# Down product of the experts' class of 112 rows: weights stationary in halves of 64 columns instead of rows stationary

## The reference, cut to what matters

```
act = clamped_swiglu(xb @ w_gu[e] + b_gu[e])     # xb: rows of the tokens of expert e
return act @ w_dn[e] + b_dn[e]                   # the "down product" is act @ w_dn[e]
```

## Time and profile before

| | us |
|---|---|
| median of 3 runs (2195.15 to 2198.58) | 2197.89 |
| profiled execution | 2196.53 |
| its span, first to last instruction | 2194.9 |
| TensorE busy | 2136.4 (97%) |
| VectorE busy | 995.7 (45%) |
| GpSimd busy | 596.6 (27%) |
| ScalarE busy | 383.1 (17%) |

### The profile page before, as it was taken

The page is one execution under the profiler, slowest core; times in us unless marked ns, Lnnn a source line. Parts: engine busy times, 40 slices in busy tenths (PEclk is TensorE's granted clock), DMA queues, the critical chain, the costliest instruction groups (busy, mean ns, idle before and its releaser), DMA issues.

```text
span 2194.9 us, 50020 instructions
## 1 busy us (share of the span) xinstructions
PE 2136.4 (97%) x20106; PEld 1655.6 (75%) x20106; DVE 995.7 (45%) x2147; ACT 383.1 (17%) x785; POOL 596.6 (27%) x905
## 2 busy tenths in 40 slices
PE   8999999999799999999999999899999999999998
PEld 5555566544488878788787789798999999999443
DVE  4665467445754434444344332623233333343474
ACT  3120066401411111011111100100000000000344
POOL 0466678200123131221311311213111232212420
PEclk9999999999899999999999999999999999999999
DMA  5100011411299999999999984988666888885740
GB/s 208 44 26 6 6 59 45 182 58 67 104 387 416 419 415 358 353 358 340 341 335 336 336 295 171 374 329 340 249 224 240 293 307 313 312 315 190 263 171 39
DMA packets 101814, 528.15 MB, mean 241 GB/s; under 512 B 22327, under 2 KB 26215, under 8 KB 49615
## 3 DMA queue, kind: packets, MB, share of 16 engines
q1 hardware_dynamic: 76894, 465.58, 56.7%
q0 software_dynamic: 24816, 61.12, 7.9%
HBM read 496.06 MB, written 27.30 MB: 238 GB/s over the span
## 4 chain that ended last, share of the span: by engine, by line
PE 91%; DVE 3%; issue 3%; ACT 2%; DMA 1%; POOL 1%; POOLq 0%; DVEq 0%; SPq 0%; ACTq 0%
PE ps L1958 23%; PE ps L1955 20%; PE ps L1971 10%; PE ps L1994 10%; PE ps L1693 5%; PE ps L2031 3%; PE ps L1984 3%; PE ps L1798 3%; PE ps L1682 3%; PE ps L1805 2%; PE ps L1644 1%; PE ps L1712 1%; PE ps L1778 1%; PE ps L1746 1%; PE ps L1677 1%
## 5 line engine op out<-in xcount | busy, mean ns | idle before, releaser
L1958 PEld LDWEIGHTS ps<-xT,wg 128*64 128x64 f32 x10752 | 498.4, 138 | 27.1 <-issue 27.1
L1958 PE MATMUL ps<-xT,wg 128*64 128x112 f32 (+5 forms) x10752 | 503.7, 257 | 12.4 <-issue 9.1
L1955 PE MATMUL ps<-xT,wg 128*128 128x144 f32 (+5 forms) x3072 | 434.8, 304 | 0.0
L1955 PEld LDWEIGHTS ps<-xT,wg 128*128 128x128 f32 x3072 | 430.0, 190 | 4.5 <-issue 1.3
L1507 DVE TENSOR_SCALAR gb<-ps,bcur 128x256 f32<-128x256 f32 x264 | 127.6, 484 | 651.2 <-PE ps L1958 377.9
L917 ACT ACTIVATE sg<-gb 128x256 f32<-128x256 f32 x264 | 110.1, 417 | 1032.9 <-DVE gb L1507 1032.9
L1971 PE MATMUL ps<-actT,wd 128*128 128x144 f32 (+5 forms) x1536 | 218.3, 304 | 0.0
L1971 PEld LDWEIGHTS ps<-actT,wd 128*128 128x128 f32 x1536 | 215.3, 190 | 1.6
L1994 PE MATMUL ps<-wd,actT 128*128 128x512 f32 x480 | 210.0, 595 | 0.0
L636 POOL DMA_INDIRECT xg<-normalised_rows,rowc x184 | 178.1, 968 | 76.6 <-issue 49.2
L1994 PEld LDWEIGHTS ps<-wd,actT 128*128 128x128 f32 x480 | 90.0, 190 | 109.9 <-issue 108.8
(11 more groups left out here) (417 smaller groups left out, 2140.9 us busy)
## 6 DMA issues: line engine op xcount, KB each, us to landing
wg<-in_w_gu SPq DMA_DIRECT2D x264, 1024.0 KB, 7.3
wd<-in_w_dn SPq DMA_DIRECT2D x132, 1024.0 KB, 7.6
expert_rows<-yb POOLq DMA_DIRECT2D x60, 128.0 KB, 5.0
expert_rows<-yb POOLq DMA_DIRECT2D x28, 160.0 KB, 5.4
hT<-in_x_cm SPq DMA_DIRECT2D x8, 512.0 KB, 9.0
cumb<-gate_sums SPq DMA_DIRECT2D x4, 1024.0 KB, 4.7
x<-in_x_tm SPq DMA_DIRECT2D x1, 4096.0 KB, 13.7
wout<-in_w_out SPq DMA_DIRECT2D x1, 4096.0 KB, 20.9
```

The costliest lines, as they stand in the source:

```text
L1955: ins = m.matmul(ps[:, f % 2, g_ * W:g_ * W + w], wg[:, f, k, g_, :], xT[:, k, 0:w], start=(k == 0), stop=(k == KT - 1))
L1958: ins = m.matmul(ps[c:c + 64, f % 2, g_ * W:g_ * W + w], wg[:, f, k, g_, c:c + 64], xT[:, k, 0:w], start=(k == 0), stop=(k == KT - 1))
```

## The change

The class of 112 rows uses the turned form of the down product: weights stationary, activations moving, result transposed out by VectorE and stored by GpSimd in the turned form. Other than in the classes over 128 rows, each block of 128 weight columns is loaded as two halves of 64. Classes 120 and 128 keep the old form.

```diff
+TURNED = (112,) + tuple(w for w in WIDTHS if w > P)
 def store_kind(w):
-    return ("groups" if w <= 96 else "rows" if w <= P else "turned", -(-w // 32))
+    return ("groups" if w <= 96 else "turned" if w in TURNED else "rows", -(-w // 32))
 def turn_kind(w):
-    return 0 if w <= P else -(-w // 32)
+    return -(-w // 32) if w in TURNED else 0
...
-                    if w <= P:
+                    if w not in TURNED:
                         y_out(b, D if w > 96 else 256 * -(-w // GR))
...
-                    v.transpose(yt[:, 0:4], yp[:, 0:4])
-                    v.transpose(yt[:, 4:blocks], yp[:, 4:blocks]).then_inc(S("y_evac"), 1)
+                    ins = v.transpose(yt[:, 0:4], yp[:, 0:4])
+                    if blocks > 4:
+                        ins = v.transpose(yt[:, 4:blocks], yp[:, 4:blocks])
+                    ins.then_inc(S("y_evac"), 1)
...
-                if w > P:
+                if w in TURNED:
+                    cols = P if w > P else 64
                     for f in range(FT):
...
                         for o_ in range(8):
-                            ins = m.matmul(ps[:, 2 + o_ // 2, W * (o_ % 2):W * (o_ % 2) + w], wd[:, f, P * o_:P * o_ + P],
-                                           actT[:, f, 0:w], start=(f == 0 and o_ % 2 == 0), stop=(f == FT - 1), skip_group_check=True)
+                            for c in range(0, P, cols):
+                                ins = m.matmul(ps[c:c + cols, 2 + o_ // 2, W * (o_ % 2):W * (o_ % 2) + w], wd[:, f, P * o_ + c:P * o_ + c + cols],
+                                               actT[:, f, 0:w], start=(f == 0 and o_ % 2 == 0), stop=(f == FT - 1), skip_group_check=True)
```

## The result

The changed kernel takes 2180.97 us (median of 4, 2178.74 to 2182.88) against 2196.73 before on the same chip: ratio 0.9926, interval 0.9914 to 0.9938, so 13.6 to 18.9 us faster. Forecast were 2185.5 and a range from 2182.0 to 2192.0: the direction was right, the gain of 15.8 us larger than the 11 forecast, and the time lies 1.0 us under the range. Two later rounds beside the kernel before gave 0.9918 (0.9905 to 0.9931) and 0.9922 (0.9908 to 0.9935).

The account below looks back on a forecast made before the run. TensorE (PE) was taken to bound the kernel. Down product -12.7, longer loop +0.5 and moved stops +0.8 made -11.4 us from the profiled 2196.53, so 2185.1, put at 2185.5 between two bases; range 2182 to 2192.

Parts of the forecast that it names:

- What bounds the kernel: Whole kernel: TensorE (PE), busy 97% of the span; a class-112 pass of 38.61 us lasts as long as its two products.
- the readout: End of class-112 down product: VectorE's 1.25 us transpose replaces ScalarE's copies and hides under the next pass; cost nothing.
- the transfers: DMA in class-112 passes: weight chunks still land in time, needed 33.9 us after being asked for; cost nothing.
- backlog: DMA work left from class 96, 7 MB, said to drain at 45 GB/s over four of the eight class-112 passes.
- The down product on PE: Class 112: 256 records at 48.2 ns, 12.34 us instead of 13.93; gain 1.59 us a pass, 12.7 in all.
- cheap bound: Class-112 down product by class 192's ratio, entry and exit free: at most 0.2 us a pass more, 14.3 in all.
- Code: Instruction fetch: 0.5 us lost once to the longer class-112 loop, 0.8 to moved stops in classes 64 and 80.
- Sum: Whole kernel: -12.7 + 0.5 + 0.8 = -11.4 us, forecast 2185.5 us; the forecast's chance 0.80.
- A: Rival, class-112 passes: transfers take part of the gain, leaving 1.16 us a pass, 9.3 in all; 2188.5 us, chance 0.08.
- C: Rival, class-112 down product: pairs do not overlap, 96.4 ns a record, +10.8 us a pass; 2283 us, chance 0.02.
- B: Rival, class-112 loop: longer body fetched anew every pass, 2223 us, or 2201 with the jump's stop alone; chance 0.10.

Follow-up runs that it names:

- full-width version: Changed kernel, but class 112's down product with full 128-column stationary tiles instead of halves of 64: 2199.21 us (12 runs), ratio 1.0003 to the kernel before.
- the version with the places of before: Changed kernel with class 128's 512-column down matmuls each split into two of 256, returning later code to its former packet places: 2182.97 us, ratio 0.9929.
- the quarters' passes: Changed kernel, but class 112's weights loaded in quarters of 32 columns instead of halves of 64: 2300.5 us in one run, beside 2198.22 for the kernel before.

## Why the prediction was wrong

- **What bounds the kernel, the readout, the transfers**: right. PE without a hole, the transpose under cover with 1.69 us to spare, 365 to 376 GB/s where 370 to 375 were said, a fourth pass of backlog. (One reading was off: of the later passes before, that from 934.71 moved 347 GB/s, not 357 to 360; nothing rested on it.)
- **The down product on PE**: this is the step that failed. The mechanism was right, the term mis-sized: 12.7 us were booked, 14.47 measured. The price of 48.2 ns a record was taken from 24.69 / 512 and so held the changes of tile width at both ends of the gate-and-up product, which the changed kernel no longer pays; and the gate-and-up product was taken to stay as it was. Without a change of tile width both products cost 24.53 / 512 = 12.27 / 256 = 47.9 ns. The sum then is 8 x (0.15 + 1.66). The prediction had this as its "cheap bound", 0.2 us a pass for entry and exit, 14.3 us in all, and gave it no cause and no place in the middle value.
- **Code**: this term failed too. +0.5 us were added for the longer body, but the first class-112 pass has no stop and takes 36.85 against 36.80, and the 0.05 lie in its gate-and-up product (24.58 for 24.53), which comes from class 96's tiles of 32 columns. +0.8 us were added for stops that move. The stops of classes 64 and 80 did move, to the record, but no cost of it shows in the scatter: the first pass from which the stops were priced took 31.98 us and was the slowest of three of the same kernel.
- **Sum**: -14.5 for -11.4 by the stretches that repeat, 3.1 of the 4.4 us by which the profiled spans went past the forecast sum (15.8 for 11.4). The other 1.3 are parts that scatter: start +0.36, class 96's first pass +1.69, class 64's -1.85, class 80's -0.70, the tail -0.80. The range ended at a bound of the passes and left no room for this scatter: by the stretches that repeat alone the profiled time would be 2196.53 - 14.52 = 2182.0, at that bound.
- **Rivals**: A did not come about (share 0.96 at 365 GB/s and no wait), C neither (the down part takes 12.27 us, not near 25). B is true of a longer body only.

Left open: the ratios all give 1 to 3.5 us more than the passes account for (only the second one's interval excludes the passes' 14.5), and the sums of the table say the same (before 865.3 to 869.0, changed 863.5 to 865.2). The full-width version is some 3.5 us better than its passes as well. The place in the packet does not explain it, since the version with the places of before sums to 864.0. Nor does the clock by itself: class 96's first pass had a mean of 0.93, 0.95 and 0.92 in the changed kernel's three profiles, against 0.96, 0.93 and 0.93 before. Nothing here shows what does.

## What to carry to other kernels

Price a product from the start of one record to the next, away from its edges, and price the edges apart: where neighbouring products use stationary tiles of one width, nothing is lost between them, and a change between 64 and 128 columns costs 0.17 us here on average. With 112 moving columns in float32, load the weights in halves (12.27 us against 14.47 with full tiles); with 120 and 128, halves were compared with the old form alone, and at 128 they gained nothing. And before a loop body grows, count its instructions against the longest body that the trace shows to be fetched once.

## What the runs showed of the hardware that was not expected

- A full-width stationary tile holds a record at 111.7 ns with 112 moving columns (113.0 with its edges), though classes 144 and 192 give 122.5 and 162.5 ns, a line that leads to 95.8 and on which class 136 still lies with 115.8. The same work in two halves costs 2 x 47.9. This is a mean: in the changed kernel's trace the records of two halves start 6 or 7 ns apart and the next two some 96 ns after them, so the two halves run side by side.
- A loop body of 2048 matmuls and weight loads is fetched anew in every pass, one of 1536 is not.
- In the quarters' passes PE stood still again and again for up to 5.6 us, and the mean granted clock of a pass was 0.87 to 0.94, so part of it ran at the lower of its two levels, 1.2 instead of 2.4 GHz; the changed kernel's class-112 passes, without stops, had 1.00. Some of the price of fetching code is this: after the stop at the jump back, 497 records of gate-and-up took 25.3 to 26.5 us, where 24.53 x 497 / 512 makes 23.8.
